# Stage borders by token block in one program section, with a ring of four weight slots

## The chip, the cores and the metric

One core of a Trainium2 chip runs the kernel. Its engines are named as in the profile: PE (matrix), DVE (vector), ACT (scalar), POOL (GpSimd) and SP, which only issues DMAs here. The metric is device time in microseconds (us), the median of the runs.

## The reference

1024 prompt tokens and 64 sample tokens, each a vector of D = 1024, go through two layers. Layer 0 mixes by gated linear attention (GLA, 4 heads, chunks of 64 tokens), layer 1 by sliding-window attention with a sink per head (SWA, 16 query heads, 4 key and value heads, two chunks of look-back). Around each mixer and each MLP stand two rms norms:

```python
h = rms_norm(x, norm_g[i, 0])
o = mixer(h)                                   # gla (i == 0) or swa (i == 1)
x = x + rms_norm(o, norm_g[i, 1])
h = rms_norm(x, norm_g[i, 2])
x = x + rms_norm(squared_relu_mlp(h, mlp_w_up[i], mlp_w_down[i]), norm_g[i, 3])
# squared_relu_mlp: square(relu(h @ w_up)) @ w_down, with D_FF = 4096
# rms_norm: x * rsqrt(mean(x * x over the 1024 features) + 1e-6) * g
```

Outputs are x for both requests, the GLA states and the SWA caches. The sample request starts from a given state and cache.

## The kernel before

Everything lies features first: a tile is 128 features by all tokens, and x, y (a mixer's or MLP's output) and h (the normed input of the next stage) have KT = 8 tiles each. The 1088 tokens are padded to 1092 and cut into NB = 3 blocks of BW = 364 columns, one PSUM bank each. A dense product is done in three passes, since h and the weights are each split into a high and a low part: w_hi by h_hi, w_hi by h_lo, w_lo by h_hi. `dense_part` (matmul at L187) issues for one input tile nine matmuls, three passes over three banks, so an output tile of an input of eight tiles is 72 matmuls over two sets of three banks that alternate.

Weights come in units of 128 x 1024. The before kernel has two slots for each of w_raw, w_hi and w_lo (`WeightStream`); SP loads w_raw, POOL makes w_hi (L138) and w_lo (L141) in the MLPs and in SWA, and in GLA ACT makes w_hi (L150) and POOL w_lo (L156).

The program is a row of sections, each with its own queue for every engine and a barrier at its end: constants, GLA, MLP0, SWA, MLP1, result. A section begins with a `Norm` and ends with a `SquareSums`:

- `SquareSums`: ACT squares y tile by tile (L508), POOL and DVE add the eight squares (L515, L525), PE sums them over the features (L531).
- `Norm` of the next section: `inverse_rms` (L392 to L399: variance, square root on ACT at L319, reciprocal, a diagonal of the result), `spread` on PE (L369) puts the factor on all partitions in PSUM, `scale` on DVE (L405) multiplies y with it, `add_to_x` (L413) adds the old x, on POOL but for the first tile. ACT makes h_hi (L327) and squares the new x (L329), DVE makes h_lo (L447) and adds the squares (L348). The second rms, of x, is not multiplied into h; the first dense product's result is scaled with it when it leaves PSUM (`mlp_norm_keep`, `swa_norm_keep`). In GLA, which has no previous y, the norm is applied to h (L317 squares, L323, L418).
- x itself goes through DRAM (`x_scratch`) between sections.

Every step of a norm works on whole tiles of 1092 columns, in the order of the tiles, so the first matmul of a stage starts when tile 0 of h is done, and PE then follows DVE and ACT tile by tile with the first of two output tiles (`before_second_tile` for the second).

In an MLP, groups of four up tiles and their part of all eight down tiles alternate, eight times (L665 square of the relu on ACT, L667 a_hi, L687 a_lo on DVE, L691 adds a down tile to y on DVE). In GLA, heads come one after the other; a head's dense work (values, projections, gate, and the output product of the head before, `output_tile`, added at L1200) is put between the small matmuls of its chunk pairs. After the last pair of head 3 its output is turned (L845), scaled, split (L1192) and multiplied with the output weights for all eight tiles. In SWA a Fori runs over query tiles; scores, softmax (L1653, L1786 to L1795), turning (L1561), values (L1570) and dense work alternate by chunk, the last output tile's eight products come behind the last chunk (L1780 adds them), and at its start y is zeroed and given the output bias (L1773).

## Time and profile before

| | us |
|---|---|
| median of 3 runs | 2883.42 |
| lowest and highest | 2877.20, 2884.84 |
| the profiled execution | 2879.99 |
| its span in the trace | 2878.2 |
| PE busy | 2627.4 (91%) |
| DVE, ACT, POOL busy | 1240.9, 671.9, 991.7 |

The span lies 1.8 us below the time of the same execution, and that execution 3.4 us below the median. The page gives totals by engine and the costliest groups; stretches of a fixed length show what one part of the program holds; waits and the timeline show who ended an engine's idle time. The granted clock is the mean of PE's two levels, 1.2 and 2.4 GHz, over a stretch: 1.00 is all at the higher one.

### The profile page before, as it was taken

Reading aid. Unit: us, or ns where it says so; the run is one execution under the profiler, and the core shown is the slowest. Engines: PE = TensorE matmul, PEld = TensorE weight load, DVE = VectorE, ACT = ScalarE, POOL = GpSimd, SP = SyncE. Lnnn points to the kernel's source line nnn. Section 1 sums busy time; section 2 is a strip of 40 time slices with the busy share of each in tenths; the row PEclk is TensorE's granted clock in tenths of the full one; section 3 lists DMA queues with packets and bytes.
Section 4 is the critical chain, followed back from the end, with each engine's and each line's share of the span. In section 5 each row is a group of like instructions: output and inputs, shape, how many; then the busy total and the mean of one; then the engine's idle time right before and its main releaser. Section 6 shows DMA issues by size and latency. Waiting matters only on the chain. (4 is left out here: it accounts for less than half of the span.)

```text
span 2878.2 us, 39586 instructions
## 1 busy us (share of the span) xinstructions
PE 2627.4 (91%) x15628; PEld 2503.2 (87%) x15628; DVE 1240.9 (43%) x2582; ACT 671.9 (23%) x1425; POOL 991.7 (34%) x393
## 2 busy tenths in 40 slices
PE   3989898986899999999996899999599999999996
PEld 2878787865899999999995888988499999999996
DVE  4464746576422322232227366666732223222323
ACT  3343334333100110011012255545211001100111
POOL 4111111116544444444446311111634444444445
PEclk9999999987899999999997999999799999999998
DMA  2000101003111111111103000000311111111113
GB/s 103 30 29 23 43 23 36 30 26 131 45 45 44 44 44 44 43 43 43 43 32 150 30 23 22 23 22 15 147 37 44 44 44 44 44 44 44 44 44 124
DMA packets 45773, 139.01 MB, mean 48 GB/s; under 512 B 9712, under 2 KB 13296, under 8 KB 45680
## 3 DMA queue, kind: packets, MB, share of 16 engines
q1 hardware_dynamic: 42544, 136.09, 13.6%
q10 hardware_dynamic: 3136, 1.65, 0.2%
q8 instruction: 63, 1.03, 0.1%
q14 instruction: 30, 0.25, 0.0%
HBM read 118.26 MB, written 19.45 MB: 48 GB/s over the span
## 5 line engine op out<-in xcount | busy, mean ns | idle before, releaser
L138 POOL TENSOR_TENSOR w_hi<-w_raw,all_ones 128x1024 fp32r<-128x1024 f32 x150 | 365.4, 2436 | 1257.8 <-PE banks L187 1212.1
L187 PE MATMUL banks<-h_hi,w_hi 128*128 128x364 f32 x2208 | 516.0, 343 | 60.3 <-DVE h_lo L447 54.7
L187 PE MATMUL banks<-h_lo,w_hi 128*128 128x364 f32 x2208 | 495.6, 333 | 0.0
L187 PE MATMUL banks<-h_hi,w_lo 128*128 128x364 f32 x2208 | 494.3, 332 | 0.0
L187 PEld LDWEIGHTS banks<-h_hi,w_hi 128*128 128x128 f32 x2208 | 385.3, 193 | 83.8 <-issue 37.6
L187 PEld LDWEIGHTS banks<-h_lo,w_hi 128*128 128x128 f32 x2208 | 392.0, 192 | 0.0
L691 DVE TENSOR_TENSOR y<-banks,y 128x1092 f32<-128x1092 f32 x128 | 165.9, 1296 | 523.4 <-PE banks L187 523.4
L187 PEld LDWEIGHTS banks<-h_hi,w_lo 128*128 128x128 f32 x2208 | 391.0, 191 | 0.0
L141 POOL TENSOR_TENSOR w_lo<-w_raw,w_hi 128x1024 fp32r<-128x1024 f32 x150 | 368.0, 2454 | 11.8
L665 ACT ACTIVATE mlp_act<-mlp_relu 128x1092 f32<-128x1092 f32 x64 | 71.9, 1123 | 1259.6 <-DVE mlp_relu L683 1259.6
L187 PE MATMUL banks<-mlp_a_hi,w_hi 128*128 128x364 f32 x1536 | 340.0, 329 | 0.0
L187 PE MATMUL banks<-mlp_a_lo,w_hi 128*128 128x364 f32 x1536 | 339.1, 329 | 0.0
L187 PE MATMUL banks<-mlp_a_hi,w_lo 128*128 128x364 f32 x1536 | 337.5, 328 | 0.0
L187 PEld LDWEIGHTS banks<-mlp_a_hi,w_hi 128*128 128x128 f32 x1536 | 265.5, 188 | 3.2 <-DVE y L691 2.7
L683 DVE SCALAR_TENSOR_TENSOR mlp_relu<-banks,mlp_norm_keep 128x1092 f32<-128x1092 f32 x64 | 82.9, 1295 | 425.7 <-PE banks L187 407.4
L187 PEld LDWEIGHTS banks<-mlp_a_hi,w_lo 128*128 128x128 f32 x1536 | 266.4, 188 | 0.0
L187 PEld LDWEIGHTS banks<-mlp_a_lo,w_hi 128*128 128x128 f32 x1536 | 266.2, 188 | 0.0
L156 POOL TENSOR_TENSOR w_lo<-w_raw,w_hi 128x1024 fp32r<-128x1024 f32 x30 | 75.2, 2508 | 515.9 <-ACT w_hi L150 515.9
L687 DVE TENSOR_TENSOR mlp_a_lo<-mlp_act,mlp_a_hi 128x1092 fp32r<-128x1092 f32 x64 | 166.5, 2602 | 148.9 <-ACT mlp_a_hi L667 148.9
L1780 DVE TENSOR_TENSOR y<-banks,y 128x364 f32<-128x364 f32 x192 | 91.1, 530 | 39.8 <-PE banks L187 39.2
L1570 PE MATMUL banks<-swa_probs,swa_v_tok 128*128 128x128 f32 (+1 forms) x512 | 96.5, 297 | 2.1 <-ACT swa_o L1678 2.0
L1570 PEld LDWEIGHTS banks<-swa_probs,swa_v_tok 128*128 128x128 f32 (+1 forms) x512 | 74.6, 195 | 14.9 <-issue 6.1
(233 smaller groups left out, 3310.6 us busy)
## 6 DMA issues: line engine op xcount, KB each, us to landing
w_raw<-in_units SPq DMA_DIRECT2D x180, 512.0 KB, 3.3
x_scratch<-mlp_norm_x SPq DMA_DIRECT2D x16, 546.0 KB, 2.7
swa_norm_x<-x_scratch SPq DMA_DIRECT2D x8, 546.0 KB, 6.9
x_scratch<-swa_norm_x SPq DMA_DIRECT2D x8, 546.0 KB, 2.7
mlp_norm_x<-x_scratch SPq DMA_DIRECT2D x8, 546.0 KB, 7.6
result_x<-x_scratch SPq DMA_DIRECT2D x8, 546.0 KB, 6.8
gla_norm_x<-in_x_prompt SPq DMA_DIRECT2D x8, 512.0 KB, 6.1
mlp_norm_x<-in_x_prompt SPq DMA_DIRECT2D x8, 512.0 KB, 5.8
```

The costliest lines, as they stand in the source:

```text
L138: hi = nc.gpsimd.tensor_tensor(c.w_hi[:, s].rearrange("p (k m) -> p k m", k=KT), raw, ones, ALU.mult)
L141: lo = nc.gpsimd.tensor_tensor(c.w_lo[:, s], c.w_raw[:, s], c.w_hi[:, s].bitcast(F32), ALU.subtract)
L156: c.nc.gpsimd.tensor_tensor(c.w_lo[:, s], c.w_raw[:, s], c.w_hi[:, s].bitcast(F32), ALU.subtract).then_inc(self.ready, 1)
L187: mm = chip.nc.tensor.matmul(chip.banks[:, 3 * s + b, 0:BW], w, x[:, k, b * BW:(b + 1) * BW], start=(k == 0 and n == 0), stop=(k == n_k - ...
L665: nc.scalar.activation(act2[:, j % 2], relu[:, j % 2], ACT.Square).then_inc(squared, 1)
L683: nc.vector.scalar_tensor_tensor(out=blocks_of(relu[:, j % 2]), in0=chip.psum_set(j % 2), scalar=0.0, in1=blocks_of(norm.keep[:]), op0=ALU ...
L687: nc.vector.tensor_tensor(a_lo[:, j], act2[:, j % 2], a_hi[:, j].bitcast(F32), ALU.subtract).then_inc(a_ready, 1)
L691: nc.vector.tensor_tensor(blocks_of(chip.y[:, m]), chip.psum_set(m % 2), blocks_of(chip.y[:, m]), ALU.add).then_inc(y_added, 1)
L1570: mm = nc.tensor.matmul(out_bank, v_tok[0:n, i, v_tile], probT[0:n, slot(c), j], start=(j == 0), stop=(j == len(parts) - 1))
L1780: nc.vector.tensor_tensor(chip.y[:, m, cols], chip.banks[:, 3 * s + b, 0:BW], chip.y[:, m, cols], ALU.add).then_inc(y_added, 1)
```

## The change

Nearly the whole file is rewritten. What it does:

- There is one section for the whole program and no barrier; stages are objects, and a `Border` stands between two of them. x is one input and y one output of 1088 columns.
- The 1088 columns are cut into blocks of 384, 384 and 320, without padding.
- The last wave of a stage (the eight output tiles of the last down group, of GLA's last head, of SWA's last query tile) goes block by block: 24 end jobs, each into one bank of 384 columns. DVE adds each into y, ACT squares it, DVE adds the squares, and PE does the sums and the spread of block b between the jobs of block b + 1. The norm's steps run by block in the same order.
- y is scaled in place and holds the new x after POOL has added the old x. x comes into four small slots and goes back to DRAM by ACT's queue.
- The first wave of the next stage goes by block too: 12 jobs, four output tiles for each block, gated by that block's h.
- The weight ring has four slots; w_raw and w_lo share their place. w_hi is made by ACT everywhere, w_lo by POOL, the first four units of a stage between POOL's adds of x.
- The start goes by block: squares, norm, rank product, and head 0's k, q and values.
- In GLA, four of head 2's output tiles move behind head 3's last pair (`late_outs`), and the first add into y is a copy. The masks are 8-bit. In SWA the loop over query tiles is written out, the output bias is added with the first product, the last tiles' output products stand at other chunks, and eight of the last wave's jobs stand between the last chunks.

The core of the diff:

```diff
-        norm = Norm(chip, "gla_norm", None, 0, x_parts=x_parts)
-        gla(chip, "gla", everything, norm)
-        norm.close()
...
-        result(chip, "result", (outs["y_prompt"], outs["y_sample"]))
+        stages = (gla, mlp0, swa, mlp1)
+        with nc.Block() as block:
...
+                chip.stream.load_rest(sp)
+                borders[4].store_all(sp, outs["y"], y_out)
...
+BLOCKS = ((0, 384), (384, 768), (768, T))
...
+class WeightStream:
+    def load_rest(self, sp):
+        with sp.Fori(1, N_UNITS // SLOTS) as i:
+            for s in range(SLOTS):
+                sp.wait_ge(self.used, SLOTS * i + (s - SLOTS + 1))
+                sp.dma_start(self.chip.w_raw[:, s], self.units[SLOTS * i + s]).then_inc(self.raw_in[s], 16)
...
+class Border:
+    def tensor_in_last_wave(self, pe, b, m):
+        if b and m == 1:
+            self.sums(pe, b - 1)
+        if b and m == 3:
+            self.spread(pe, b - 1)
+        if (b, m) == (2, KT - 1) and self.middle:
+            self.sums_x(pe, 0)
+    def tensor_in_first_wave(self, pe, b, j):
+        if (b, j) == (0, 0):
+            self.spread_x(pe, 0)
+            self.sums(pe, 2)
+        if (b, j) == (0, 1):
+            self.spread(pe, 2)
+            self.sums_x(pe, 1)
+        if (b, j) == (0, 2):
+            self.spread_x(pe, 1)
...
+    def high(self, act, b, k):
...
+        nc.scalar.activation(self.chip.h_hi[:, k, COLS[b]], y, ACT.Copy,
+                             scale=self.chip.gains[:, self.pre, k:k + 1]).then_inc(self.s.hi_done, 1)
...
+        nc.scalar.activation(self.s.sq_x[:, k % 2, 0:WIDTH[b]], y, ACT.Square).then_inc(self.s.squared_x, 1)
+        act.dma_start(self.chip.x_dram[:, k, COLS[b]], y).then_inc(self.s.x_out, 16)
+        if after < NB * KT:
+            self.load_x(act, after // KT, after % KT)
...
+    def step(self, dve, b, s):
+        if s < KT:
+            self.scale(dve, b, s)
...
+        if s >= 2:
+            self.low(dve, b, s - 2)
+        if s >= 3 and self.middle:
+            self.add_squares_x(dve, b, s - 2)
+    def vector_in_last_wave(self, dve, b, m):
+        self.add_squares(dve, b, m - 1)
+        if b and m == 0:
+            self.add_squares(dve, b - 1, KT - 1)
+        if b == 2 and m < 3:
+            self.step(dve, 0, m + 6)
+        if b == 2 and m == 2:
+            self.step(dve, 0, 9)
+        if b and m == 2:
+            self.inverse(dve, b - 1)
+        if b and m > 2:
+            self.step(dve, b - 1, m - 3)
+        if b and m == KT - 1:
+            self.step(dve, b - 1, KT - 3)
...
+    def gpsimd_with_units(self, pool, next_unit):
+        ws = self.chip.stream
+        self.gpsimd_block(pool, 0, 0, KT)
+        self.gpsimd_block(pool, 1, 0, 4)
+        ws.low(pool, next_unit)
+        self.gpsimd_block(pool, 1, 4, 6)
+        ws.low(pool, next_unit + 1)
+        self.gpsimd_block(pool, 1, 6, KT)
+        ws.low(pool, next_unit + 2)
+        self.gpsimd_block(pool, 2, 0, 2)
+        ws.low(pool, next_unit + 3)
+        self.gpsimd_block(pool, 2, 2, KT)
...
+    def vector_before_first_wave(self, dve):
+        self.add_squares(dve, 2, KT - 1)
+        for s in range(KT - 2, KT + 2):
+            self.step(dve, 1, s)
+        self.inverse_x(dve, 0)
+        self.inverse(dve, 2)
...
+class Mlp:
+    def tensor(self, pe):
+        for b in range(NB):
+            for j in range(FF_TILES):
...
+                for k in range(KT):
+                    if j == 0:
+                        self.before.h_ready(pe, b, k)
+                    w = slice(k * P, (k + 1) * P)
+                    mm = dense(chip, chip.banks[:, n % JOB_BANKS, 0:WIDTH[b]], chip.w_hi[:, j, w], chip.w_lo[:, j, w],
+                               chip.h_hi[:, k, COLS[b]], chip.h_lo[:, k, COLS[b]], k == 0, k == KT - 1)
...
+                self.before.tensor_in_first_wave(pe, b, j)
...
+        for b in range(NB):
+            for m in range(JOB_BANKS if b == 0 else 0, KT):
+                pe.wait_ge(self.end_added, KT * b + m - JOB_BANKS + 1)
+                for k in range(FF_TILES):
+                    mm = end_part(b, m, k)
+                mm.then_inc(self.end_full, 1)
+                if b == NB - 1 and m % 2:
+                    ws.finish()
+                self.after.tensor_in_last_wave(pe, b, m)
```

## Rows read from the trace of the kernel before

**Rows 1.** Totals of the page: busy us, share of the span, instructions

```profile
PE 2627.4 (91%) x15628; PEld 2503.2 (87%) x15628; DVE 1240.9 (43%) x2582; ACT 671.9 (23%) x1425; POOL 991.7 (34%) x393
```

**Rows 2.** Stretches of 50 us: busy (instructions) PE, PEld, DVE, ACT, POOL; PEclk, DMA, GB/s

```profile
650.00:700.00 50.00, 34.67 (x168) 31.51 (x166) 25.25 (x36) 12.96 (x13) 25.68 (x11) 0.74 0.33 117
700.00:750.00 50.00, 34.32 (x149) 31.44 (x150) 40.61 (x24) 15.13 (x15) 40.75 (x11) 0.77 0.27 105
750.00:800.00 50.00, 49.10 (x286) 47.62 (x285) 16.21 (x10) 10.21 (x11) 19.80 (x8) 0.99 0.10 33
800.00:850.00 50.00, 50.00 (x302) 50.00 (x301) 11.79 (x8) 2.23 (x2) 19.59 (x9) 1.00 0.14 46
1500.00:1550.00 50.00, 25.61 (x109) 20.17 (x107) 39.01 (x24) 19.03 (x18) 34.69 (x11) 0.76 0.48 190
1550.00:1600.00 50.00, 43.03 (x216) 41.20 (x217) 20.54 (x15) 5.39 (x9) 29.04 (x11) 0.83 0.12 38
1600.00:1650.00 50.00, 42.32 (x222) 39.23 (x221) 17.54 (x30) 12.53 (x43) 11.93 (x5) 0.86 0.10 32
2000.00:2050.00 50.00, 28.41 (x123) 24.47 (x123) 37.75 (x45) 19.31 (x18) 24.87 (x9) 0.69 0.37 145
2050.00:2100.00 50.00, 35.19 (x162) 31.87 (x162) 32.77 (x19) 10.68 (x13) 31.61 (x9) 0.83 0.17 66
```

**Rows 3.** PE's waits: us in total, times, longest

```profile
PE banks L187 <- DVE h_lo L447: 54.7, 24, 8.1
PE banks L357 <- DVE gla_norm_work L348: 21.9, 1, 21.9
...
PE banks L821 <- POOL gla_rank_w L803: 20.9, 1, 20.9
...
PE banks L1561 <- DVE swa_probs L1795: 10.6, 10, 3.2
```

**Rows 4.** Timeline: start us, us, engine line operation, count, [idle before <-releaser]

```profile
120.74 0.27 PE L904 MATMUL banks<-identity,gla_work 128*128 128x128 f32 x1
...
635.54 0.64 PE L944 MATMUL banks<-gla_v_tok,gla_att 64*64 64x256 f32 x2
...
649.41 1.25 PE L187 MATMUL banks<-gla_o_hi,w_hi 128*128 128x364 f32 x3 [3.20 <-DVE gla_o_lo L1192]
...
1502.83 0.66 PE L187 MATMUL banks<-mlp_a_hi,w_lo 128*128 128x364 f32 x3
...
1526.61 1.25 PE L187 MATMUL banks<-h_hi,w_hi 128*128 128x364 f32 x3 [8.00 <-DVE h_lo L447]
...
2848.20 4.00 PE L531 MATMUL banks<-all_ones,mlp_more_squares 128*128 128x1 f32 x18 [3.86 <-DVE mlp_more_squares L525]
...
2853.20 1.50 DVE L399 TENSOR_TENSOR result_diag<-identity,result_rs 128x512 f32<-128x512 f32 x3
...
2861.42 0.34 SPq L308 DMA_DIRECT2D out_y_prompt<-result_x  x1
```

**Rows 5.** Single lines: count, ns min/median/max, first and last start us, forms

```profile
L418 DVE TENSOR_TENSOR h_lo<-gla_norm_work,h_hi x4: 1289/1292/1294, 37.0 to 48.2; 128x1092 fp32r<-128x1092 f32 x4
...
L447 DVE SCALAR_TENSOR_TENSOR h_lo<-swa_norm_x,gains,h_hi x8: 2351/2360/3420, 1523.9 to 1547.8; 128x1092 fp32r<-128x1092 f32 x8
...
L687 DVE TENSOR_TENSOR mlp_a_lo<-mlp_act,mlp_a_hi x64: 1296/2622/2723, 760.9 to 2800.0; 128x1092 fp32r<-128x1092 f32 x64
...
L405 DVE SCALAR_TENSOR_TENSOR swa_norm_work<-y,gains,banks x8: 1337/1340/1352, 1518.7 to 1540.6; 128x1092 f32<-128x1092 f32 x8
...
L508 ACT ACTIVATE mlp_more_squares<-y x8: 1112/1120/1124, 1486.9 to 2845.7; 128x1092 f32<-128x1092 f32 x8
...
L413 POOL TENSOR_TENSOR swa_norm_x<-swa_norm_x,swa_norm_work x7: 2492/3579/3592, 1522.8 to 1543.0; 128x1092 f32<-128x1092 f32 x7
```

**Rows 6.** The page's costliest groups: busy us, mean ns, idle before

```profile
L141 POOL TENSOR_TENSOR w_lo<-w_raw,w_hi 128x1024 fp32r<-128x1024 f32 x150 | 368.0, 2454 | 11.8
...
L1780 DVE TENSOR_TENSOR y<-banks,y 128x364 f32<-128x364 f32 x192 | 91.1, 530 | 39.8 <-PE banks L187 39.2
```

More of the change, by code:

```diff
@@ L178, in dense_part, with dense, dense_set @@
+def dense(chip, out, w_hi, w_lo, x_hi, x_lo, first, last):
+    for n, (w, x) in enumerate(((w_hi, x_hi), (w_hi, x_lo), (w_lo, x_hi))):
+        mm = chip.nc.tensor.matmul(out, w, x, start=(first and n == 0), stop=(last and n == 2))
+        if n == 0:
+            chip.stream.tell_used(mm)
+    return mm
+def dense_set(chip, s, k, n_k, at, slot, hi, lo, before_bank=None):
     w_hi, w_lo = chip.w_hi[:, slot, at:at + P], chip.w_lo[:, slot, at:at + P]
@@ L182, in dense_part @@
         order = [(n, b) for b in range(NB) for n in range(3)]
-    for n, b in order:
+    for i, (n, b) in enumerate(order):
         w, x = passes[n]
@@ L351, in sum_squares @@
-    def sum_squares(self, pe, n):
-        tile, n_adds = self.totals[n]
-        pe.wait_ge(self.sq_added.sem, self.sq_added.at(n_adds))
-        for j, t in enumerate(self.TOK):
-            mm = self.chip.nc.tensor.matmul(self.chip.banks[:, self.SUM_BANK, j:j + 1], self.work[:, tile, t:t + P],
-                                            self.chip.ones[:, 0:1], start=(n == 0 and j == 0),
-                                            stop=(n == len(self.totals) - 1 and j == self.N_TOK - 1))
-        mm.then_inc(self.sq_used.sem, 1)
@@ L362, in spread @@
-    def spread(self, pe, n, piece, bank):
-        pe.wait_ge(self.diag_done.sem, self.diag_done.at(NB * n + piece + 1))
-        if piece < 2:
-            width, rhs = 4 * P, self.diag[:, 4 * piece:4 * piece + 4]
-        else:
-            width, rhs = TP - SEQ, self.diag[:, 8, P - (TP - SEQ):P]
-        self.chip.nc.tensor.matmul(self.chip.banks[:, bank, 0:width], self.chip.ones[:], rhs,
-                                   start=True, stop=True).then_inc(self.rs_full.sem, 1)
-    def tensor(self, pe):
-        if self.first:
-            self.sum_squares(pe, 0)
-        for piece in range(NB):
-            self.spread(pe, 0, piece, self.RS_BANK + piece)
@@ new lines, in keep_block, with scalar_before_last_wave @@
+    def keep_block(self, act, b):
+        act.wait_ge(self.s.keep_full, self.per_pre(1) + b + 1)
+        self.chip.nc.scalar.copy(self.chip.keep[:, COLS[b]], self.chip.banks[:, KEEP_BANK, 0:WIDTH[b]]
+                                 ).then_inc(self.s.kept, 1)
+    def scalar_before_last_wave(self, act):
+        before = self.shared if self.middle else self.added
+        if before:
+            act.wait_ge(self.s.x_out, 16 * NB * KT * before)
+        for k in range(self.X_SLOTS):
+            self.load_x(act, 0, k)
@@ L1707, in _ @@
[L1707 to L1718 removed]
+                for stage in stages:
+                    stage.scalar(act)
```

3217 lines of the change are left out of this document (1788 added, 1429 removed).

## The prediction

> **What bounds the kernel now.** I read the page's totals first. TensorE (PE) is busy 91% of the span [rows 1]: the kernel is bound by matmuls, and what can be won is PE's idle time and the time in which its clock is low. So next I read the stretches of 50 us: a stretch inside an MLP holds 302 matmuls at clock 1.00, that is 50 / 302 = 0.1656 us for one of 364 columns; the stretches around the changes of stage hold 109 to 286 at a mean granted clock of 0.69 to 0.99 [rows 2]. Missing matmuls times 0.1656 us is what a border costs: GLA to MLP0 134 + 153 + 16 = 303, or 50 us, and 14 us more from 635.5 to 649.4 while head 3's output is turned and normed [rows 2, 4]; MLP0 to SWA 193 + 86 = 279, or 46 us, and 13 us at SWA's start (80); SWA to MLP1 179 + 140 = 319, or 53 us. The list of PE's waits says who is late there: DVE's low part of h 24 times, the first squares, the split of the rank weight [rows 3]. Last I read PE's timeline for marks: scores of GLA's first pair begin at 120.7, MLP0's last matmuls end at 1503.5, SWA's first starts at 1526.6, and the last norm's sums start at 2848.2, 30 us before the end [rows 4].
>
> **Prices.** A DVE operation that adds a bank to y takes 0.53 us on 364 columns, less back to back; I take 0.48 [rows 6]. The scale with its factor in PSUM takes 1.34 on 1092, so 0.49 on a block [rows 5]. A DVE operation with two inputs in SBUF takes 1.29 on 1092 where POOL is idle and 2.36 to 2.62 where POOL works [rows 5]: 0.48 or 0.87 on a block. The new borders have POOL adding x and splitting weights, but not all the time, so I take 0.65. An rms (three small operations and the diagonal, 1.50 for three blocks, which has two SBUF inputs) I put at 1.5 with its handovers to ACT and PE [rows 4]. POOL: 2.49 alone and 3.58 contended per 1092 columns of x, so 0.83 to 1.2 a block; 2.45 for a w_lo [rows 5, 6]. ACT: 1.12 per 1092 columns, 0.40 a block; a DMA's issue 0.34 by the row on SP's queue [rows 4, 5].
>
> **A middle border, part by part (MLP0 to SWA).** The code puts all end adds, sums of squares, scales, low parts and second sums on DVE: per border 24 of each. Alone that is 24 x (0.48 + 0.49 + 3 x 0.48) = 58 us, plus six rms, with little waiting 63; all contended 92; at 0.65 it is 24 x (0.97 + 1.95) = 70 plus 9, or 79, and 12 reads of the first wave's banks add 6. PE has 288 matmuls in the last wave (47.7 us), 288 in the first (47.7) and some 6 us of sums and spreads: 101 us. ACT has 24 x (3 x 0.40 + 2 x 0.34) = 45 us with its x stores and loads, and fits. In the last wave DVE must do 24 x (0.48 + 0.65) = 27, block 0's rms and eight steps of 1.79, 15.8, and five steps of block 1, 9: 52 us against PE's 47.7, so DVE sets the pace there. Then 47.7 + 6. Added waits stop PE in order: the second spread of block 0 stands behind the first job of the new stage and waits for an rms queued behind four steps of block 1 (6 to 8 us; every later job waits behind it); the sums and spread of block 1 inside the last wave (3); the first w_lo behind POOL's adds (3); the fourth w_lo behind two adds of block 2, which need a spread that PE does after its second job (2 to 3). That is 16: 52 + 54 + 16 = 122. PE's clock is low for some us after each stop of several us (0.76 in 1500 to 1550 [rows 2]): 7. So 129 us, where the kernel before takes 95.4 + 9 of sums (4.0 at the end of the kernel [rows 4]) and spreads + 46 idle = 150.6: **21.6 us gained**. Bounds: 106 without a stop, 141 with every DVE pair contended. At SWA's start bias adds, their waits and memsets go and the second query tile fills PE: 8 of the 13 us (4 to 13).
>
> **GLA to MLP0.** GLA's last wave is only 144 matmuls, 24 us of PE work, so DVE's 52 stands alone; four output tiles now lie under the turning of head 3 (6 of its 14 us stay idle). Idle after: 6 + 28 + 10 = 44 of 64: **20** (5 to 40). **SWA to MLP1.** The last wave is 72 matmuls, 12 us of PE work, of which block 0's third moves under attention chunks; DVE's 52 sets it, so 53 becomes 41: **11.5** (0 to 30).
>
> **The start.** x lands, is squared and normed by block, the rank weight no longer waits behind weight splits (20.9 us), the first sums no longer for all of x (21.9) [rows 3]. Before the scores PE has head 0's two projections (144 matmuls, 23.8 us), its values (216 of 256 columns, by columns 0.116 each, 25), the gate and the rank product (some 15); block 0 is ready at about 24, block 2 at about 55, DVE and ACT doing 24 scales and low parts. With 64 us of work, most of it after block 0, the last third waiting for block 2, the scores start at about 106 instead of 120.7 [rows 4]: **14** (6 to 20).
>
> **The end.** Of 30 us after the last matmul [rows 4], square, sums, rms, scale and x add now run over 320 columns, not 1092; the stores of blocks 0 and 1 go earlier. One block's eight scales and four adds are 6.5 us, rms and spread 4, squares and handovers 5, the store about 3, and DVE is a few us behind: 22. **8** (6 to 13).
>
> **The rest.** 1088 columns for 1092 is 0.37% of 12,384 x 0.1656 = 2051 us, less the borders: **6.4**. In GLA and SWA w_hi leaves POOL, and y's zeroing and masks shrink; SWA's probabilities stopped PE for 10.6 us [rows 3] while POOL split weights: 6, and 3 in GLA: **9** (0 to 15). The move of w_hi to ACT inside the MLPs I cost at nothing: ACT has two operations per up tile there, 2.2 of some 12 us; without that cover each would cost 1.1 us.
>
> **Sum.** 21.6 + 8 + 20 + 11.5 + 14 + 8 + 6.4 + 9 = 98.5. The profiled execution took 2880.0 with a span of 2878.2; 2880.0 - 98.5 = 2781.5. The median of the runs, 2883.4, is 3.4 above that execution, so the forecast is 2785.
>
> **A rule against it.** The low part took 2.36 while POOL's x add took 3.58 instead of 2.49 [rows 5]: both grow, by about 1.1. The Trainium skill ("SBUF — State Buffer", section "Who interferes with whom") says that DVE with two SBUF inputs and GpSimd share a port as an exclusive lock, and that the second to issue is blocked for the whole of the first. By that a short DVE operation that meets a w_lo would lose up to all of it; The row shows both sides slowed, neither stopped for the whole of the other; no row has a short DVE operation against a long POOL one at a border. It is the third case below.
>
> **Rivals.**
> DVE keeps up. The pairs stay near 0.48 because POOL's 24 adds and 4 splits (30 us) fill less than a third of 100 us. The last waves of DVE fall from 52 to 41: 11 us in two borders, 4 in the third, where PE bounds; stops halve (7 x 3), low-clock stretches go (17), the end gains 4 more: 68 us, **2717**. For it: the low part at the start took 1.29 beside an idle POOL [rows 5]. Against: POOL follows DVE step by step, so they run together just when DVE is pressed.
>
> DVE is blocked. Each POOL operation stops DVE for its length: 24 x 0.83 + 4 x 2.45 = 30 us a border, where I took 24 x 3 x 0.17 = 12. 18 x 3 = 54, of which 52/85 lie where DVE sets the pace: 33, **2818**. Against it: the row above, where DVE lost 1.07 and not 2.49.
>
> Weights late. A slot is refilled only when the stage's last wave finishes with it; then load, ACT copy and POOL split follow, the split behind x adds. If each of the first four jobs waits some 4 us, three borders lose 45: **2830**. For it: the last waves of GLA and SWA free slots within a few us of their end. Against: a job of the first wave, 24 matmuls, lasts 4 us, and only the first two units have none ahead of them.
>
> Slower: PE's low clock. The rows show 0.69 and 0.74 in the stretches with stops [rows 2]. If the stops in front of jobs (a wait for a spread or a block of h before nearly every one) keep PE at 1.2 GHz through the three first waves and MLP0's last, 4 x 47.7 = 191 us of work doubles, less 55 of low clock and stops counted or hidden by it and of what DVE's pace covers (20): about 115 us, **2900**. [...] Against: 2050 to 2100 holds many short stops at 0.83.
>
> **How the numbers follow.** Forecast 0.45, DVE keeps up 0.20, blocked 0.12, weights late 0.11, low clock 0.07, and 0.05 for a mix of the last three with nothing at start and end. The first four are all faster by over 0.3%, which is about what a measurement can tell; the fifth is slower; of the rest 0.01 is faster, 0.03 the same and 0.01 slower: 0.89, 0.03, 0.08. Lower bounds of the forecast together (10 + 4 + 5 + 0 + 6 + 6 + 6 + 0) give 2846, upper ones (45 + 13 + 40 + 30 + 20 + 13 + 7 + 15) 2700; all at once is unlikely, so 2705 to 2840, which takes in the second to fourth cases.
>
> **What would show it.** Right: 302 to 305 matmuls in 50 us inside MLPs; PE's waits led by DVE's low part and sums at borders, 25 to 45 us idle at each; DVE near full in last waves; low part near 0.65 a block; scores at about 106; some 22 us after the last dense matmul. Wrong: DVE's low part at 0.48 (second case) or over 1 (third); waits for w_lo at the top (fourth); first waves at clock 0.5 (fifth). What would break the sum most is a chain at the borders through ACT or PE in order that I left out, or queue order that hides more than I gave it.

## The result and the profile after

| | before | after |
|---|---|---|
| median of the runs, us | 2882.56 | 2834.72 |
| lowest and highest | 2877.20, 2884.84 | 2827.68, 2843.70 |
| the profiled execution | 2879.99 | 2830.92 |
| its span | 2878.2 | 2829.0 |

The ratio is 0.984 (95% interval 0.981 to 0.987). The kernel became faster by 48 us, where 98 were forecast: the sign is right, the time lies in the range, and the gain is a little under half of the forecast's.

The page's totals of after, which answer to [rows 1]: PE works 31 us less, but it still stands idle for 232 us (2829.0 - 2596.7), 19 less than before.

```profile
PE 2596.7 (92%) x15574; PEld 2477.6 (88%) x15574; DVE 1218.8 (43%) x3140; ACT 860.1 (30%) x1854; POOL 541.6 (19%) x271
```

To see where the time went, both traces are cut at the same marks: the first scores of GLA; the first scores of head 3; the add of the first down tile of MLP0's first group that follows the border; the last add of its seventh group; SWA's first row maximum; that of its last query tile; the two adds in MLP1; the end. For after, the columns are length, busy us (instructions) of PE, PEld, DVE, ACT, POOL, then PE's granted clock, DMA share and GB/s:

```profile
0.00:114.80 114.80, 79.79 (x456) 69.95 (x457) 51.54 (x140) 46.90 (x88) 12.93 (x11) 0.91 0.24 80
114.80:543.20 428.40, 390.36 (x2538) 349.76 (x2537) 253.48 (x1110) 156.94 (x300) 57.12 (x22) 0.97 0.10 31
543.20:818.90 275.70, 227.23 (x1285) 207.97 (x1284) 175.97 (x491) 95.22 (x193) 66.05 (x40) 0.91 0.18 59
818.90:1392.50 573.60, 573.60 (x3458) 572.10 (x3457) 128.58 (x169) 100.69 (x96) 118.86 (x48) 1.00 0.14 45
1392.50:1595.30 202.80, 179.86 (x1022) 175.11 (x1020) 99.74 (x167) 69.96 (x135) 56.44 (x36) 0.92 0.25 78
1595.30:1911.70 316.40, 298.24 (x1833) 269.89 (x1834) 189.92 (x529) 176.18 (x682) 30.92 (x13) 0.99 0.07 23
1911.70:2134.00 222.30, 173.13 (x944) 162.48 (x945) 134.08 (x266) 87.44 (x225) 56.16 (x36) 0.86 0.20 64
2134.00:2707.60 573.60, 573.60 (x3458) 572.10 (x3458) 128.59 (x170) 100.67 (x96) 118.87 (x48) 1.00 0.14 45
2707.60:2829.00 121.40, 100.92 (x595) 98.27 (x593) 56.92 (x105) 26.07 (x40) 24.21 (x17) 0.93 0.28 89
```

Length less PE's busy time is PE's idle time. In the records of the lower clock (1.2 GHz) dense matmuls of 384 columns start every 0.32 us, in those of the higher (2.4 GHz) every 0.17 to 0.18; so about half of the busy time in records of the lower clock is lost as well, and half is what the table takes. The table has both ("idle + low clock") for the same stretches of the two traces:

| stretch | before: length, idle + low clock | after | gain | forecast |
|---|---|---|---|---|
| start, to GLA's first scores | 120.7, 46.9 + 0 | 114.8, 35.0 + 7.5 | 5.9 | 14 |
| GLA, to head 3 | 423.7, 35.7 + 6.0 | 428.4, 38.0 + 9.2 | -4.7 | 3 |
| head 3 to MLP0's first down tile | 286.7, 50.5 + 23.6 | 275.7, 48.5 + 16.1 | 11.0 | 20 |
| MLP0 and MLP1 inside | 1152.6, 0 + 0 | 1147.2, 0 + 0 | 5.4 | 6.4 |
| MLP0 to SWA's first row maximum | 230.6, 37.9 + 16.9 | 202.8, 22.9 + 10.4 | 27.8 | 29.6 |
| SWA inside | 318.4, 11.8 + 9.8 | 316.4, 18.2 + 2.9 | 2.0 | 6 |
| SWA's last tile to MLP1's first down tile | 215.6, 41.7 + 18.5 | 222.3, 49.2 + 16.7 | -6.7 | 11.5 |
| end | 129.9, 26.3 + 3.5 | 121.4, 20.5 + 1.4 | 8.5 | 8 |
| sum | | | 49.2 | 98.5 |

Three terms came as forecast: columns, MLP0 to SWA, the end. The missing 49 us lie in two borders (9 and 18), in the start (8), and in GLA and SWA inside (8 and 4). The border SWA to MLP1 is longer than before.

Where in a border after loses it: the last wave, from DVE's first end add to its last, and the rest of the stretch, for the borders to MLP0, SWA and MLP1 (same columns):

```profile
645.40:696.10 50.70, 32.17 (x160) 30.04 (x159) 43.58 (x80) 23.34 (x48) 13.72 (x12) 0.80 0.31 97
696.10:818.90 122.80, 107.86 (x609) 105.19 (x610) 58.63 (x94) 35.97 (x69) 40.23 (x24) 0.91 0.22 69
1446.20:1503.00 56.80, 48.01 (x271) 46.54 (x269) 44.42 (x80) 23.10 (x48) 17.60 (x15) 0.94 0.32 98
1503.00:1595.30 92.30, 78.16 (x429) 74.87 (x429) 44.25 (x74) 33.23 (x75) 28.95 (x19) 0.87 0.26 83
1952.70:2009.30 56.60, 26.80 (x120) 22.13 (x118) 47.14 (x91) 30.31 (x75) 14.76 (x13) 0.72 0.25 77
2009.30:2134.00 124.70, 109.33 (x609) 106.65 (x610) 58.70 (x94) 36.10 (x69) 39.05 (x23) 0.91 0.21 68
```

Idle time and low clock together are 24.2, 12.2 and 36.0 us in the three last waves, and 21.0, 21.2 and 23.0 us behind them.

Stretches of 50 us of after, same columns, beside [rows 2]. The MLP now takes 303 matmuls of at most 384 columns; the border to SWA has 167 and 297 where it had 109 and 216; around 2000 the counts are still 117 and 143 at clocks of 0.75 and 0.74, with DVE busy for 77 to 79%:

```profile
650.00:700.00 50.00, 28.43 (x141) 26.30 (x140) 44.70 (x78) 24.06 (x49) 17.62 (x14) 0.78 0.34 106
700.00:750.00 50.00, 38.86 (x191) 36.84 (x190) 36.57 (x61) 20.46 (x44) 19.54 (x15) 0.81 0.25 80
...
800.00:850.00 50.00, 50.00 (x303) 50.00 (x303) 10.71 (x14) 7.38 (x7) 8.72 (x4) 1.00 0.13 43
1500.00:1550.00 50.00, 35.54 (x167) 34.10 (x167) 36.41 (x56) 18.82 (x38) 23.25 (x16) 0.76 0.32 103
1550.00:1600.00 50.00, 47.86 (x297) 45.29 (x296) 13.53 (x33) 18.74 (x50) 9.12 (x5) 1.00 0.18 60
...
1950.00:2000.00 50.00, 25.81 (x117) 21.24 (x118) 39.72 (x82) 26.48 (x71) 9.45 (x8) 0.75 0.24 74
2000.00:2050.00 50.00, 31.16 (x143) 29.37 (x142) 38.40 (x57) 20.48 (x40) 23.71 (x16) 0.74 0.27 85
```

What PE waits for in after (us in total, times, longest), which answers to [rows 3]. DVE's low part of h, first there with 54.7, is gone but for one wait of 2.3 at the start. In its place stand the rms steps (sums L316, spreads L325 and L342) and the split of weights:

```profile
PE banks L316 <- DVE norm_acc L455: 47.5, 8, 16.1
PE banks L342 <- DVE norm_diag_x L504: 30.8, 3, 11.0
...
PE banks L325 <- DVE norm_diag L504: 23.4, 9, 5.9
PE banks L182 <- POOL w_lo L159: 19.3, 6, 7.8
...
PE banks L202 <- POOL w_lo L159: 7.5, 1, 7.5
```

PE's timeline at the border SWA to MLP1, the longer stops alone (start, us, engine, line, operation, [idle before <- releaser]): the sums of block 1, its spread, the first w_lo, the second spread of block 0. These four are 33.6 us of the stretch's 49.2 idle:

```profile
1989.35 1.44 PE L316 MATMUL banks<-all_ones,norm_acc 128*128 128x1 f32 x6 [8.85 <-DVE norm_acc L455]
...
1998.49 1.65 PE L325 MATMUL banks<-norm_diag,all_ones 128*128 128x384 f32 x2 [5.90 <-DVE norm_diag L504]
...
2011.16 0.69 PE L182 MATMUL banks<-h_hi,w_hi 128*128 128x384 f32 x1 [7.84 <-POOL w_lo L159]
...
2028.61 1.65 PE L342 MATMUL banks<-norm_diag_x,all_ones 128*128 128x384 f32 x2 [10.97 <-DVE norm_diag_x L504]
```

The same four stops are 9.55, 4.44, 5.93 and 9.39 us at the border to MLP0 and 4.50, 1.64, 3.99 and 10.47 at the border to SWA. From DVE's last add of an end job to the second spread of block 0, 19.5, 19.3 and 19.3 us pass at the three borders, and DVE is busy for 19.2, 19.0 and 18.9 of them: a queue of DVE work that is as long behind a last wave of 72 matmuls as behind one of 288. It is called the queue below.

**What DVE does in it.** DVE's and POOL's timelines in the same place:

```profile
2007.55 1.34 DVE L469 TENSOR_TENSOR norm_acc_x<-norm_sq_x 128x384 f32<-128x384 f32 x1
2008.82 0.48 DVE L1508 TENSOR_TENSOR y<-banks,y 128x320 f32<-128x320 f32 x1
2009.22 2.24 DVE L455 TENSOR_TENSOR norm_acc<-norm_acc,norm_sq 128x320 f32<-128x320 f32 x1
```
```profile
2007.24 1.24 POOL L569 TENSOR_TENSOR y<-y,norm_x 128x384 f32<-128x384 f32 x1 [1.01 <-DVE y L516]
2008.44 2.67 POOL L159 TENSOR_TENSOR w_lo<-w_raw,w_hi 128x1024 fp32r<-128x1024 f32 x1
```

The add of squares on 320 columns takes 2.24 us beside a split that ends at 2011.11, and ends 0.35 us after it. The one on 384 columns takes 1.34 beside an x add that ends at 2008.48, and ends 0.41 after it. Between the two an add that reads PSUM takes 0.48, although the split is running. DVE lines of the whole trace (count, ns min/median/max):

```profile
L469 DVE TENSOR_TENSOR norm_acc_x<-norm_acc_x,norm_sq_x x54: 477/1163/1367, 671.9 to 2062.3; 128x384 f32<-128x384 f32 x36, 128x320 f32<-128x320 f32 x18
```
```profile
L1508 DVE TENSOR_TENSOR y<-banks,y x24: 476/548/558, 1952.7 to 2008.8; 128x384 f32<-128x384 f32 x16, 128x320 f32<-128x320 f32 x8
```
```profile
L516 DVE SCALAR_TENSOR_TENSOR y<-y,gains,banks x120: 530/601/617, 22.6 to 2824.2; 128x384 f32<-128x384 f32 x80, 128x320 f32<-128x320 f32 x40
```

Operations with one input in PSUM (L1508, L516) never grow. The add with two inputs in SBUF has a median of 1.16 us. Of its 54 executions 30 begin inside a POOL operation, and each of these ends 0.34 to 0.42 us after that operation; the other 24 take 0.48 to 0.55. A border has 66 operations with two inputs in SBUF on whole blocks (21 adds of each kind of square, 24 low parts) and they take 54 to 55 us, some 0.83 each; the forecast had 0.65. In the queue of the border to MLP1, three that meet a split (2.24, 2.67, 2.69) and four that meet an x add (1.34 to 1.36) take 9.2 us more than their own 0.48 to 0.60: nearly half of its 19.3.

**The start.** PE's first two operations, ACT's queue, and the last stop before the scores:

```profile
16.12 1.41 PE L316 MATMUL banks<-all_ones,norm_acc 128*128 128x1 f32 x6 [16.12 <-DVE norm_acc L455]
20.90 1.65 PE L325 MATMUL banks<-norm_diag,all_ones 128*128 128x384 f32 x2 [3.36 <-DVE norm_diag L504]
```
```profile
8.39 4.38 ACTq L290 DMA_DIRECT2D y<-in_x  x7
...
14.76 3.75 ACTq L290 DMA_DIRECT2D y<-in_x  x8
```
```profile
109.62 1.25 PE L202 MATMUL banks<-h_hi,w_hi 128*128 128x384 f32 x3 [7.55 <-POOL w_lo L159]
```

ACT issues 16 loads of x, eight in the middle of block 0's squares (the row shows the last seven) and eight ahead of its square root; these issues hold ACT's queue for over 8 us while PE waits. The stop of 7.55 is the fifth weight unit: its raw weights were there, but ACT's copy stands in its queue behind value copies and exponentials and starts at 106.0.

### The profile page after: what moved, and what is told of

Same layout as the page of the kernel before. It is cut to its first block, busy times and chain, and to the rows that moved or that the text cites. A ratio compares the mean times of both kernels' runs of the same rounds, so it can differ in the third digit from the quotient of the medians.

```text
span 2829.0 us, 39614 instructions
## 1 busy us (share of the span) xinstructions
PE 2596.7 (92%) x15574; PEld 2477.6 (88%) x15574; DVE 1218.8 (43%) x3140; ACT 860.1 (30%) x1854; POOL 541.6 (19%) x271
## 3 DMA queue, kind: packets, MB, share of 16 engines
q8 instruction: 79, 1.29, 0.2%
## 4 chain that ended last, share of the span: by engine, by line
PE 78%; DVE 14%; ACT 4%; issue 3%; ACTq 1%; DMA 0%; POOL 0%; SPq 0%; DVEq 0%; POOLq 0%
PE banks L202 54%; PE banks L182 12%; PE banks L1724 3%; PE banks L1193 2%; DVE norm_acc_x L469 2%; DVE norm_acc L455 2%; PE banks L1173 1%; PE banks L1824 1%; DVE gla_att L2268 1%; DVE y L516 1%; DVE y L1474 1%; PE banks L1184 1%; DVE h_lo L528 1%; DVE swa_prob L1490 1%; PE banks L1859 1%
## 5 line engine op out<-in xcount | busy, mean ns | idle before, releaser
L202 PE MATMUL banks<-h_hi,w_hi 128*128 128x384 f32 x1872 | 428.0, 337 | 9.8 <-POOL w_lo L159 7.5
L202 PE MATMUL banks<-h_lo,w_hi 128*128 128x384 f32 x1872 | 414.1, 329 | 0.0
L202 PE MATMUL banks<-h_hi,w_lo 128*128 128x384 f32 x1872 | 413.5, 329 | 0.0
L152 ACT CAST w_hi<-w_raw 128x1024 fp32r<-128x1024 f32 x180 | 186.7, 1045 | 454.9 <-DMA w_raw<-in_units 452.8
L898 DVE TENSOR_TENSOR y<-banks,y 128x768 f32<-128x768 f32 x192 | 130.0, 719 | 401.6 <-PE banks L202 400.0
L202 PE MATMUL banks<-mlp_a_hi,w_hi 128*128 128x384 f32 (+1 forms) x1344 | 296.6, 329 | 1.5 <-issue 1.3
L202 PE MATMUL banks<-mlp_a_lo,w_hi 128*128 128x384 f32 (+1 forms) x1344 | 295.1, 327 | 0.0
L202 PE MATMUL banks<-mlp_a_hi,w_lo 128*128 128x384 f32 (+1 forms) x1344 | 295.0, 327 | 0.0
L182 PE MATMUL banks<-h_hi,w_hi 128*128 128x384 f32 (+1 forms) x360 | 132.4, 368 | 20.5 <-POOL w_lo L159 17.8
L182 PE MATMUL banks<-h_lo,w_hi 128*128 128x384 f32 (+1 forms) x360 | 126.7, 352 | 0.0
L182 PE MATMUL banks<-h_hi,w_lo 128*128 128x384 f32 (+1 forms) x360 | 125.9, 350 | 0.0
```

Of the source, the lines that this page charges most:

```text
L152: self.chip.nc.scalar.copy(self.chip.w_hi[:, s], self.chip.w_raw[:, s]).then_inc(self.hi_done, 1)
L182: mm = chip.nc.tensor.matmul(out, w, x, start=(first and n == 0), stop=(last and n == 2))
L202: mm = chip.nc.tensor.matmul(chip.banks[:, 3 * s + b, 0:WIDTH[b]], w, x[:, k, COLS[b]], start=(k == 0 and n == 0), stop=(k == n_k - 1 and ...
L898: op = nc.vector.tensor_tensor(y, bank, y, ALU.add)
```

## The experiments

Two theories stood against each other. **A: the lock.** A DVE operation with two inputs in SBUF waits for the whole rest of a POOL operation that it meets; DVE's queue grows by that, and PE stops behind it. **B: amount and order.** DVE is slow because it has too much to do, and PE stops because small steps (an rms) are queued behind bulk; who blocks whom matters little. Every ratio below is against the kernel before in the same session; after has 0.984 (0.981 to 0.987). The four runs of after itself lie between 2827.7 and 2843.7 us, so differences between kernels of less than some 7 us are not read.

**The x adds on DVE.** POOL keeps only the four splits of each middle border.

```diff
+        if s < KT and self.middle:
+            self.add_x(dve, self.chip.nc.vector, b, s)
...
-        self.gpsimd_block(pool, 0, 0, KT)
-        self.gpsimd_block(pool, 1, 0, 4)
-        ws.low(pool, next_unit)
...
+        for i in range(4):
+            ws.low(pool, next_unit + i)
```

> The x adds of the three middle borders go from POOL to DVE (72 operations of about 0.55 us), and POOL keeps only the four weight splits. Theory A, DVE sets the pace at the borders and its operations with two SBUF inputs are stopped by POOL's for their whole length: the second sums of squares (line 469 in the changed kernel, 1.34 us each beside a running x add, 0.55 without) fall to about 0.55, which pays for the 24 x 0.55 = 13 us of added work per border, the splits are done earlier, and PE's waits for w_lo at the first jobs (17.8 us in three borders) fall under 6: 10 to 20 us faster than the changed kernel, 2815 to 2825. Rival, DVE is only overloaded by its number of operations: 13 us more per border, 25 to 40 slower, 2860 to 2875.

Measured: 2827.9 us, ratio 0.982 (0.979 to 0.985). Without POOL's x adds the line falls to its undisturbed time, but for the meetings with a split (2.72):

```profile
L469 DVE TENSOR_TENSOR norm_acc_x<-norm_acc_x,norm_sq_x x54: 481/551/2722, 675.2 to 2059.7; 128x384 f32<-128x384 f32 x36, 128x320 f32<-128x320 f32 x18
```

The x adds were what made it slow. Yet the time doesn't move beyond the noise, and neither guess of it came true: the adds cost DVE 14.5 us a border, and it wins 13 to 15 us of waiting in the 66 pair operations. PE's waits for w_lo at L182 fall from 19.3 us to 6.1, but those for the second diagonal rise from 30.8 to 47.7. The Trainium skill ("Perfetto Trace Analysis", section "Optimizing Scalar/DVE Operations") says that moving work between DVE and GpSimd might not help, since they share a port: here nothing is won either way.

**Few columns.** The adds of the second squares read 8 columns instead of a block, all but the first add of each block; the second rms leaves out the rest.

```diff
+        n = n if k == 1 else 8
```

> DVE's second sums of squares are cut to 8 columns for all but the first of each block, so the norm of x is left incomplete; the number and the order of operations stay. Theory A (a DVE operation with two SBUF inputs waits for the whole POOL operation that runs): those beside an x add fall only from 1.34 to about 0.9 us, since the wait stays; about 9 us of DVE per border, 10 to 15 us faster than the changed kernel in all. Rival (both only run slower side by side): they fall to under 0.2 us, some 18 us of DVE per border, and the time falls by 30 to 40 us.

Measured: 2813.4 us, 0.975 (0.973 to 0.978).

```profile
L470 DVE TENSOR_TENSOR norm_acc_x<-norm_acc_x,norm_sq_x x54: 152/837/991, 683.9 to 2057.9; 128x8 f32<-128x8 f32 x54
...
683.56 1.24 POOL L570 TENSOR_TENSOR y<-y,norm_x 128x384 f32<-128x384 f32 x1 [2.02 <-DVE y L517]
683.87 0.95 DVE L470 TENSOR_TENSOR norm_acc_x<-norm_acc_x,norm_sq_x 128x8 f32<-128x8 f32 x1
```

Of the 54 adds 24 begin outside any POOL operation and take 0.152 to 0.163 us; 30 begin inside an x add (1.05 in the median) and take 0.84 to 0.99, and every one of the 30 ends 0.02 to 0.03 us after that x add. The time is not the operation's work but a wait for the rest of POOL's. That is the mechanism of theory A by itself. The Trainium skill ("SBUF — State Buffer", section "Who interferes with whom") calls the port pair that DVE and GpSimd share an exclusive lock, and says that a DVE instruction with two SBUF inputs contends with a GpSimd instruction that reads SBUF; the trace agrees, and the operations of L516 and L1508, which have one in PSUM, are free of it. The time fell by 21 us, between theory A's 10 to 15 and the rival's 30 to 40; it is the durations that decide. The low parts, which now meet the x adds instead, grow from a mean of 0.69 to 0.76 at the three borders to one of 0.76 to 0.83.

**Later spreads.** PE's hooks in the first wave come one job later, and the fourth split ahead of block 2's x adds.

```diff
-        if (b, j) == (0, 0):
+        if (b, j) == (0, 1):
             self.spread_x(pe, 0)
             self.sums(pe, 2)
-        if (b, j) == (0, 1):
+        if (b, j) == (0, 2):
             self.spread(pe, 2)
             self.sums_x(pe, 1)
...
-        self.gpsimd_block(pool, 2, 0, 2)
         ws.low(pool, next_unit + 3)
-        self.gpsimd_block(pool, 2, 2, KT)
+        self.gpsimd_block(pool, 2, 0, KT)
```

> PE does the second spread of block 0 and what follows it one job later in the first wave, and POOL does the fourth split before the x adds of block 2. Rival B, the order on PE costs the time: the wait for the second spread's diagonal (30.8 us in three borders) falls to about 15, and the time by 10 to 15 us. Theory A, DVE's queue is what is late: the wait moves to later spreads and to the first job of block 2, and the time stays within 6 us.

Measured: 2830.5 us, 0.981 (0.978 to 0.984). The wait for the second diagonal falls from 30.8 to 17.2 us, that for the second sums rises from 3.8 to 9.2, that for w_lo from 19.3 to 21.4: PE's order alone moves about half of the stop elsewhere, since DVE's queue ahead of it stays (19.4 to 19.6). PE's idle time falls by 5.6 us, its low clock takes 6.1 more, and the median doesn't move beyond the noise.

**The first splits on ACT.** In place of the low part of the first four units ACT puts a copy of their high part, so their low part is left out.

```diff
+    def low_by_scalar(self, act, unit):
+        c, s = self.chip, unit % SLOTS
+        act.wait_ge(self.hi_done, unit + 1)
+        c.nc.scalar.copy(c.w_lo[:, s], c.w_hi[:, s].bitcast(F32)).then_inc(self.ready, 1)
...
-        ws.low(pool, next_unit)
...
         if (b, m) == (2, 6):
             self.chip.stream.high(act, next_unit + 1)
+            self.chip.stream.low_by_scalar(act, next_unit + 1)
```

> The first four units of a middle border get a copy of the high part by ACT as their low part, in place of POOL's subtraction: the low part of these weights is left out, and POOL has only x adds. Theory A: the DVE operations of 2.2 to 2.7 us (five a border beside a split, 2.1 us above their own 0.55) vanish, so some 10 us of DVE per border, and PE's waits for w_lo (17.8 us in three) with them: 30 to 45 us faster than the changed kernel, 2790 to 2805. Rival C, only the weights are late: 15 to 20 us faster, and the DVE's durations stay.

Measured: 2817.5 us, 0.977 (0.975 to 0.980).

```profile
L533 DVE SCALAR_TENSOR_TENSOR h_lo<-y,gains,h_hi x72: 539/606/1293, 664.9 to 2044.1; 128x384 fp32r<-128x384 f32 x48, 128x320 fp32r<-128x320 f32 x24
```

In after the same line has a maximum of 2.695; here it is 1.293, and no DVE operation of a border takes 2.2 or more. The queue falls from 19.3 to 13.5. The waits for the first w_lo go, and 11.5 us of idle time, 17 of the median. The durations are those of theory A, the time is what rival C had (15 to 20): PE comes to the second spread earlier and waits longer for it (35.4 instead of 30.8 in three borders), and how much of the 17 is DVE's and how much the weights' this run doesn't part.

**Roots first.** DVE does the last square's add, then both rms of blocks 0 and 2, and only then the remaining steps of block 1; ACT and PE follow that order.

```diff
             self.sums_x(pe, 0)
+            self.sums(pe, 2)
...
+        self.root_x(act, 0)
+        self.root(act, 2)
         ws.high(act, next_unit + 2)
...
         self.add_squares(dve, 2, KT - 1)
-        for s in range(KT - 2, KT + 2):
-            self.step(dve, 1, s)
         self.inverse_x(dve, 0)
         self.inverse(dve, 2)
+        for s in range(KT - 2, KT + 2):
+            self.step(dve, 1, s)
```

> At the middle borders DVE does the second rms of block 0 and the first rms of block 2 ahead of the last four steps of block 1, ACT the two roots likewise, and PE takes the sums of block 2 at the end of the last wave. In the changed kernel 19.4 us lie between the last end add and the second spread of block 0 in each of the three borders, nearly all of it DVE's queue. If that order is what stops PE there, the 19.4 fall to about 5, the wait for the second diagonal (30.8 us in three borders) to under 6, less time at the low clock follows, and the whole is 20 to 30 us faster than the changed kernel: about 2805 to 2815. Rival, DVE's amount of work decides whatever its order: the stop moves to the first job of block 1, and the time falls by less than 10.

Measured: 2817.6 us, 0.978 (0.975 to 0.981). The wait for the second diagonal is gone from the list, but PE now stands before the sums of block 2, for the squares' adds that DVE does last:

```profile
2013.52 1.44 PE L316 MATMUL banks<-all_ones,norm_acc 128*128 128x1 f32 x6 [14.27 <-DVE norm_acc L455]
```

The waits for these sums rise from 47.5 to 85.7 us. Order, DVE's and ACT's together, is worth some 17 us, less than the 20 to 30 expected; what is left is the work that DVE must have done by then, as theory B says.

**The fifth unit early.** ACT copies unit 5 right after block 2's start.

```diff
         take_start(2, 2)
+        ws.high(act, self.unit(0, 4))
...
-            ws.high(act, self.unit(h, 4))
             if h:
+                ws.high(act, self.unit(h, 4))
```

> In head 0 ACT makes the high part of the fifth weight unit right after the last projection copy, ahead of three value copies and the first decays. If the 7.5 us for which PE waits at 102 to 109 come from ACT's order and not from the late refill of the slot, the wait vanishes, scores begin 5 to 7 us earlier than 114.8, and the low clock that follows it (10 us) goes too: 6 to 10 us faster. Rival, the refill is late: the wait stays over 4 us, and under 3 us are gained.

Measured: 2834.8 us, 0.983 (0.980 to 0.986). The stop of 7.55 is gone and the scores begin at 111.1 instead of 114.8 (4.0 of the gain go to a wait for DVE's `gla_work`). The total doesn't show it: the low clock takes 13.1 us of GLA where it took 9.2, and 18.8 instead of 16.1 at the next border.

**Squares on POOL.** POOL adds the second squares.

```diff
             self.add_x(pool, self.chip.nc.gpsimd, b, k)
+            if k >= 3:
+                self.add_squares_x(pool, self.chip.nc.gpsimd, b, k - 2)
...
-        if s >= 3 and self.middle:
-            self.add_squares_x(dve, b, s - 2)
```

> The second sums of squares (21 additions per middle border, 20 us of DVE) go from DVE to POOL. Theory A, DVE's amount of work sets the pace of the two borders with a short last wave (GLA to MLP0, SWA to MLP1): idle there falls by 7 to 10 us each and by 3 to 5 in the other, with the 19.4 us to the second spread at about 14: 15 to 30 us faster than the changed kernel. Rival, POOL with 24 + 21 additions and 4 splits (some 55 us) now stops DVE more often or is late itself: within 8 us of the changed kernel, and first parts and low parts on DVE grow.

Measured: 2817.3 us, 0.977 (0.975 to 0.980). Idle time falls at each border, from 48.5 to 43.0, 22.9 to 19.4 and 49.2 to 40.3, and the queue to 17.8. So moving work between these two can help after all, where the rule cited above says that it might not: the 21 adds take 20 to 21 us of operation and wait off DVE at each border, of which the low parts give 3 to 4.5 back (0.83 to 0.88 each), and POOL, busy for 56.16 of the 222.3 us of after's border to MLP1, has room for them.

**All three.** Roots first, the fifth unit, squares on POOL.

> The three edits before this together. If the order, the fifth unit and the squares are separate causes: 40 to 60 us faster than the changed kernel, 2775 to 2795. If the first and the third only shorten the same queue: 25 to 35 us faster.

Measured: 2801.9 us, 0.972 (0.969 to 0.975), 33 us less than after. PE's largest wait:

```profile
PE banks L316 <- DVE norm_acc L455: 70.4, 11, 15.7
```

Queue 13.8 to 14.8. The two gains of 17 add up, and the fifth unit adds nothing, as alone; the time lies in the second guess only because each gain was smaller than expected. Of the 30 us of idle time that go (232.3 to 202.3), 25 go at the three borders; they keep 42.1, 15.6 and 37.8.

**x by SP.** The start's loads of blocks 1 and 2 are issued by SP.

```diff
             before.square(act, 0, k)
-            if k == 3:
-                before.load_first_x(act, 1)
-        before.load_first_x(act, 2)
         before.root(act, 0)
...
                 chip.stream.load_first(sp)
+                borders[0].load_first_x(sp, 1)
+                borders[0].load_first_x(sp, 2)
```

> At the start SP's queue instead of ACT's issues the loads of x for the second and third block. In the changed kernel ACT issues eight loads in 4.4 us between the fourth and the fifth square of the first block, and eight more in 3.75 us ahead of the first root; the first sums start at 16.1 and the first spread at 20.9. If ACT's issues are what is late there, the sums start at about 12, the spread at about 13.5 and the dense work 6 to 8 us earlier; scores begin at about 108 instead of 114.8: 5 to 8 us faster than the changed kernel. Rival, the first block of x or the weights are late themselves: sums at 15 or later, under 2 us gained.

Measured: 2832.2 us, 0.984 (0.981 to 0.986). The first sums and spread:

```profile
12.12 1.41 PE L316 MATMUL banks<-all_ones,norm_acc 128*128 128x1 f32 x6 [12.12 <-DVE norm_acc L455]
14.82 1.65 PE L325 MATMUL banks<-norm_diag,all_ones 128*128 128x384 f32 x2 [1.29 <-DVE norm_diag L504]
```

They come 4.0 and 6.1 us earlier and the scores 4.9 (109.9), so the loads on ACT's queue cost that much there. The total is that of after: low clock takes 15.3 us of GLA instead of 9.2, and 20.2 instead of 16.7 at the border to MLP1, where nothing was changed.

**More.** All three, x by SP, ACT's second unit one step later, and step 5 of block 1 behind the rms.

```diff
-        if (b, m) == (2, 6):
+        if (b, m) == (2, 7):
             self.chip.stream.high(act, next_unit + 1)
...
+        if b and m == KT - 1 and not (b == 2 and self.middle):
             self.step(dve, b - 1, KT - 3)
```

> The order, the fifth unit, the squares on POOL and the x loads on SP together, and in the last wave the second weight copy of ACT after the last square and step 5 of block 1 after the two rms. In the run with the first three, 7 us lie between the last end add and the sums of block 2 at a middle border; they should fall to about 3.5. With 6 us at the start and 3 at each of three borders: 12 to 18 us faster than the run with three edits, 2784 to 2790.

Measured: 2798.6 us, 0.972 (0.970 to 0.974): 36 us below after and 82 below before in its own session, but the ratio is that of the run with three edits, and the time 9 to 15 above what was expected. The scores begin at 103.0, and the queue is down to 11.8 to 12.8. Idle time is 202.1 us, as much as without these edits: the start has 7.7 less, and the three borders have 5.6 more (43.7, 17.1 and 40.3). The trace shows where at each border; the one to MLP1:

```profile
1988.89 0.18 DVE L492 RECIPROCAL rs_x<-rs_x 128x3 f32<-128x3 f32 x1 [3.82 <-ACT rs_x L387]
...
1991.46 1.26 POOL L567 TENSOR_TENSOR y<-y,norm_x 128x384 f32<-128x384 f32 x1 [4.66 <-DVE y L516]
...
1996.65 0.69 PE L182 MATMUL banks<-h_hi,w_hi 128*128 128x384 f32 x1 [3.72 <-POOL w_lo L159]
```

With step 5 moved behind the rms, DVE stands idle for ACT's root, POOL waits for that step's y, and the second split stands behind that x add in POOL's queue. PE's waits for the sums of block 2 fall by 1.9 to 2.4 us, but it now waits 2.7, 3.4 and 3.7 us for the second split. The step was bulk work, but another engine's queue hung on it.

## Where the prediction was right and where it failed

**Right.** *Columns*: 5.4 in the MLPs, where 6.4 were for every dense product. *MLP0 to SWA and SWA's start*: 27.8 of 29.6; there the last wave has 288 matmuls and DVE's work lies beside PE's. Of the 27.8, 21.3 are idle time and low clock, and 6.5 are less work for PE, where the forecast had 3 (sums and spreads, 9 to 6); so that the size fits is in part luck. *The end*: 8.5 of 8. The move of w_hi to ACT inside the MLPs cost nothing: PE has no idle time there.

**Failed: what PE loses behind the last wave, at the two borders with a short one.** This is the step that cost most. For the border to SWA the forecast worked it out: second spread 6 to 8, first w_lo 3, fourth 2 to 3, low clock 7, some 20 us; 21.2 were measured. For GLA to MLP0 it had 10 for all of this (6 + 28 + 10), for SWA to MLP1 next to nothing (41 is about DVE's 52 less PE's 12). The trace has 21.0 and 23.0: the queue is the same 19.3 to 19.5 us at all three borders, and PE's second spread stands behind it. These are 33 us that the sum left out. Some 10 came back: the two last waves lost 24.2 and 36.0 where the forecast had 28 and 40, the turning of head 3 lost 3.8 for 6. So without head 3's and the last chunks' own work GLA to MLP0 fell from 60 to 49 us of idle time and low clock (forecast: 64 to 44), and SWA to MLP1 rose from 52 to 59 (forecast: 53 to 41). That the queue is what stops PE there the runs show: both rms ahead of four steps won 17 us, the squares taken off DVE another 17, both together 33.

**Failed: the size of the stops.** The forecast gave a border's second spread 6 to 8 and the first w_lo 3. Measured at the borders to MLP0, SWA and MLP1: 9.4, 10.5, 11.0 and 5.9, 4.0, 7.8. The sums and spread of block 1 had 3 at the border to SWA and took 6.1; at the other two (14.0 and 14.8) they are part of the last wave that DVE paces. The places are those that were named. The low clock is 16 us in each of these two stretches, where the border that was worked through had 7; before, it was 23.6 and 18.5.

**Failed: the price of a DVE pair operation.** The forecast took 0.65 us; a border shows 0.83 (54 to 55 us in 66 operations), near the upper bound of 0.87. The forecast had 72 of them in 47 us, so DVE has 7 to 9 us more of them in a border. The last waves show little of it: they took 51, 57 and 57 us where the forecast had 52. The queue shows it: 9.2 of 19.3 us are waits for POOL at the border to MLP1, and without the splits it is 13.5. The reason is the lock, which the forecast weighed and set aside. It argued from [rows 5] that DVE's low part and POOL's x add each grew by 1.1 us, so neither stopped for the whole of the other. The rows didn't speak against the lock: an operation that meets another in its course waits only for its rest, and where long operations alternate, each waits for a part of the other. The trace of before shows it, if one looks at ends and not at durations: the eight L447 of [rows 5] all begin inside a POOL operation and end 1.15 us after it, and so do 62 of the 64 L687; that is nearly the 1.29 that such an operation takes alone, so it waited and then ran. The 8 columns that end with POOL's operation are the proof.

**Failed: the start.** The 14 us left out that ACT issues the x loads between its squares (4.9 us, shown by giving them to SP) and that its copy of the fifth unit comes late (3.7 us, shown by moving it). They also gave the low clock nothing: PE's idle time fell by 11.9 us there, but 7.5 us go to a low clock that before doesn't have in this stretch. ACT's 45 us of work at a border were priced with its DMA issues, the start's were not.

**Failed: inside GLA and SWA.** The 9 us of *the rest* came out as -2.7. GLA has 2.3 more of idle time and 3.2 more low clock; SWA's idle time rose by 6.3 while its low clock fell by 6.9. No run took this apart.

**The rivals.** *DVE is blocked* (2818) had the mechanism, which the runs show, and the time closest to it apart from *weights late* (2830). It fell short by 17 us, since it changed the pair price alone and kept the forecast's start, low clock and order. *Weights late* came true in part: 17.8 us at three first jobs and 7.5 before the scores, of its 45. *DVE keeps up* is out: 0.83 against 0.48. *Low clock slower* is out as a whole (the first wave at SWA has clock 1.00 from 1550 on), though the low clock takes 64 us of the span, 43 of them at the three borders.

**Open.** The shares of order, lock and amount overlap, and their gains of 17 us were measured each to some 8. It wasn't tried to keep step 5 in its place with the other edits of the last run, nor to make DVE's part of the last wave smaller at the borders to MLP0 and MLP1, where some 40 us of idle time remain.

## What to carry to other kernels

When a border between stages is cut into blocks, write down for each engine the queue between the last result of one stage and the first job of the next; the steps that release the next stage (sums, rms, first weights) go ahead of bulk work on every one of them, DMA issues included. A DVE operation with two inputs in SBUF costs its own time and the rest of any POOL operation that it meets; so give POOL few, short ones, or give it whole steps of DVE's queue, and read one input from PSUM where that can be. Check a rule on blocking with the shortest operation that the trace has, or by whether one operation's end follows the other's, not by how much two long ones grow. Where stages differ in the length of their last wave, price what comes behind the wave for each of them.

## What the chip showed that was not expected

**A very short operation shows a lock best.** 8 columns took 0.15 to 0.16 us free and 0.84 to 0.99 when they began inside one of POOL's x adds, and 320 columns 2.24 beside a split of 2.67.

**Which engine begins first decides who waits.** The low part of the activation took 2.62 us in the median before [rows 5]; in after all 56 take the undisturbed time (count, ns min/median/max):

```profile
L889 DVE TENSOR_TENSOR mlp_a_lo<-mlp_act,mlp_a_hi x56: 1291/1292/1293, 833.6 to 2758.1; 128x1088 fp32r<-128x1088 f32 x56
```

In before 62 of the 64 begin inside a POOL operation. In after none of these does: a split begins 0.99 to 1.00 us after each of the 56, and it is the split that is longer, 2.55 to 2.57 us against 2.34 to 2.41 where DVE is idle. No run changed this alone. It didn't shorten the MLPs, where PE is never idle.

**The low clock's share varies where nothing was changed.** In the GLA stretch, with the same instructions, PE's idle time lay between 36.1 and 38.7 us in after and its ten relatives, but the loss to low clock between 8.9 and 23.3. Gains of 4 to 5 us at the start vanished in it twice. An earlier start of GLA alone doesn't explain it: the run that starts it first (103.0) lost 13.6 us, the one that starts it last (117.0) 18.9. What sets it these runs can't tell.
